# The last sums of c11 on GpSimd instead of VectorE at the end of each half of an MLP with seven-product multiplication

## The reference, cut to what matters

```python
hn = rmsnorm(h, norm2_g[l])
ff = jnp.square(jax.nn.relu(jnp.einsum('bsd,df->bsf', hn, w_mlp_in[l])))
h = h + jnp.einsum('bsf,fd->bsd', ff, w_mlp_out[l])
return rmsnorm(h, final_norm_g)
```

## Time and profile before

| what | value |
|---|---|
| time, median of 3 runs | 2180.83 us (2179.65 to 2180.89) |
| the profiled execution, its own time | 2179.79 us |
| its span, first to last instruction | 2178.1 us |
| PE busy | 2142.7 us (98%) |
| DVE busy | 1610.7 us (74%) |
| POOL busy | 872.0 us (40%) |
| ACT busy | 807.8 us (37%) |

### The profile page before, as it was taken

The page is one execution under the profiler, slowest core; times in us unless marked ns, Lnnn a source line. Parts: engine busy times, 40 slices in busy tenths (PEclk is TensorE's granted clock), DMA queues, the critical chain, the costliest instruction groups (busy, mean ns, idle before and its releaser), DMA issues.

```text
span 2178.1 us, 29249 instructions
## 1 busy us (share of the span) xinstructions
PE 2142.7 (98%) x9880; PEld 1755.8 (81%) x9880; DVE 1610.7 (74%) x2602; ACT 807.8 (37%) x1220; POOL 872.0 (40%) x860
## 2 busy tenths in 40 slices
PE   7999999999999999999999999999999999999998
PEld 6787788788878878888888888878788888888877
DVE  2899877887669853778678678786786786786785
ACT  4445554335165360323323333234223323323314
POOL 5553364044134432344344344434443533533521
PEclk9999999999999999999999999999999999999999
DMA  6884467355644647112112112132321121121111
GB/s 215 275 260 134 144 217 266 130 172 173 231 154 160 233 169 250 39 39 76 39 39 76 39 39 77 58 110 82 138 77 39 39 77 39 39 77 39 39 58 78
DMA packets 149822, 252.35 MB, mean 116 GB/s; under 512 B 9936, under 2 KB 91888, under 8 KB 149744
## 3 DMA queue, kind: packets, MB, share of 16 engines
q1 hardware_dynamic: 149744, 251.34, 35.0%
HBM read 205.17 MB, written 46.14 MB: 115 GB/s over the span
## 4 chain that ended last, share of the span: by engine, by line
PE 90%; DVE 4%; ACT 0%; issue 0%; POOLq 0%; POOL 0%; DVEq 0%; ACTq 0%
PE acc L75 22%; PE acc L77 22%; PE acc L76 22%; PE acc L2093 3%; PE acc L2095 3%; PE acc L2094 3%; PE acc L2138 2%; DVE h_sb L1617 2%; PE acc L1936 2%; PE acc L1937 2%; PE acc L1938 2%; PE acc L2053 1%; PE acc L2051 1%; PE acc L2052 1%; PE acc L1854 1%; PE acc L2118 1%
## 5 line engine op out<-in xcount | busy, mean ns | idle before, releaser
L954 POOL TENSOR_TENSOR up_lo<-raw_a,up_hi 128x1024 fp32r<-128x1024 f32 x62 | 149.5, 2413 | 544.2 <-ACT up_hi L1160 544.2
L1505 DVE SCALAR_TENSOR_TENSOR acc<-u_sb,cw_col,acc 128x512 f32<-128x512 f32 x464 | 313.2, 751 | 0.4
L76 PE MATMUL acc<-dn_lo,ff_hi 128*128 128x512 f32 x728 | 283.5, 389 | 0.0
L77 PE MATMUL acc<-dn_hi,ff_lo 128*128 128x512 f32 x728 | 283.5, 389 | 0.0
L75 PE MATMUL acc<-dn_hi,ff_hi 128*128 128x512 f32 x728 | 283.5, 389 | 0.0
L1658 DVE TENSOR_TENSOR h_sb<-acc,h_sb 128x512 f32<-128x512 f32 x416 | 269.3, 688 | 0.0
L1663 DVE TENSOR_TENSOR relu<-relu 128x512 f32<-128x512 f32 x104 | 74.3, 714 | 208.8 <-ACT relu L1260 208.8
L75 PE MATMUL acc<-xT_hi,wt 128*128 128x512 f32 x512 | 207.4, 405 | 1.5 <-ACT q_sb L1345 1.5
L75 PE MATMUL acc<-xT_hi,up_hi 128*128 128x512 f32 x512 | 200.1, 391 | 1.9 <-DVE h_sb L1582 1.1
L77 PE MATMUL acc<-xT_hi,wt 128*128 128x512 f32 x512 | 199.9, 390 | 0.0
L76 PE MATMUL acc<-xT_lo,wt 128*128 128x512 f32 x512 | 199.7, 390 | 0.0
(11 more groups left out here) (238 smaller groups left out, 4659.5 us busy)
## 6 DMA issues: line engine op xcount, KB each, us to landing
wt<-w_kept SPq DMA_DIRECT2D x168, 512.0 KB, 3.3
raw_a<-in_w_mlp_in SPq DMA_DIRECT2D x64, 512.0 KB, 6.9
raw_b<-in_w_mlp_out SPq DMA_DIRECT2D x62, 512.0 KB, 3.7
w_kept<-wt SPq DMA_DIRECT2D x48, 512.0 KB, 4.5
w_raw<-in_w_in SPq DMA_DIRECT2D x32, 256.0 KB, 3.6
h_sb<-h_dram SPq DMA_DIRECT2D x16, 512.0 KB, 7.0
res_sb<-in_x SPq DMA_DIRECT2D x7, 1024.0 KB, 5.5
h_dram<-res_sb SPq DMA_DIRECT2D x7, 1024.0 KB, 6.3
```

Source lines behind the costliest of these rows:

```text
L76: nc.tensor.matmul(out, w_hi, x_lo, start=False, stop=False)
L77: return nc.tensor.matmul(out, w_lo, x_hi, start=False, stop=last)
L954: nc.gpsimd.tensor_tensor(m_lo[i], raw[i], m_hi[i].bitcast(F32), ALU.subtract).then_inc(up_lo_ok, 1)
L1505: nc.vector.scalar_tensor_tensor(out=y_sb[:, j, :] if k == TAPS - 1 else bank, in0=u_sb[:, j, k:k + BLK], scalar=cw_col[:, j, k:k + 1], in ...
```

## The change

In the step after the seven-product ones POOL does the three combinations of `c11`, 12 instructions of 128 x 512 per half, right behind its two `dn_lo` and ahead of its two `up_lo`. It waits for the last of the seven-product adds (`seven_add`), which DVE has counted, and each second and third instruction of a tile for the one before it (a new semaphore, `c11_ok`). DVE does the other five combinations: 0 and 1 ahead of the first square as before, one each behind tiles 0 and 1, none behind tiles 2 and 3, and one tile of the last combination instead of two after each of the first four pairs of adds. The adds 0, 2, 4 and 6 wait for their tile of `c11`. SP waits for both semaphores ahead of the next half's loads.

```diff
+            def finish_c11(f, i):
+                half = f // NF
+                if i == 0:
+                    pool.wait_ge(seven_add, NS * (half + 1) * MT)
+                for n, (other, op) in enumerate(((m1_sum, ALU.add), (m4_sum, ALU.add), (m5_sum, ALU.subtract))):
+                    if n > 0:
+                        pool.wait_ge(c11_ok, half * 12 + 3 * i + n)
+                    nc.gpsimd.tensor_tensor(c11[i], c11[i], other[i], op).then_inc(c11_ok, 1)
...
@@ GpSimd, step(f) @@
                 for i in range(FT):
                     down_low(f, i)
                 if after_seven(f):
+                    for i in range(4):
+                        finish_c11(f, i)
                     for i in range(FT):
                         up_low(f + 1, i)
...
@@ SyncE @@
-                    sp.wait_ge(comb_ok, 32)
+                    sp.wait_ge(comb_ok, 20)
+                    sp.wait_ge(c11_ok, 12)
...
@@ VectorE, adds(f) @@
-                    if after_seven(f) and n in (0, NG // 2):
-                        dve.wait_ge(comb_ok, f // NF * 32 + (24 if n == 0 else 32))
+                    if after_seven(f) and n % 2 == 0 and t < 4:
+                        dve.wait_ge(c11_ok, f // NF * 12 + 3 * t + 3)
+                    if after_seven(f) and n == 0:
+                        dve.wait_ge(comb_ok, f // NF * 20 + 8)
+                    if after_seven(f) and n == NG // 2:
+                        dve.wait_ge(comb_ok, f // NF * 20 + 20)
...
                     if n % 2 == 1 and after_seven(f) and t < 4:
-                        combine(f, 6, [t])
-                        combine(f, 7, [t])
+                        combine(f, 4, [t])
...
@@ VectorE, combine(f, k, rows) @@
-                into, other, op = ((c22, c12, ALU.add), (c12, m5_sum, ALU.add), (c11, m1_sum, ALU.add),
-                                   (c11, m4_sum, ALU.add), (c11, m5_sum, ALU.subtract), (c22, c21, ALU.subtract),
+                into, other, op = ((c22, c12, ALU.add), (c12, m5_sum, ALU.add), (c22, c21, ALU.subtract),
                                    (c21, m4_sum, ALU.add), (c22, m1_sum, ALU.add))[k]
...
-                        dve.wait_ge(comb_ok, f // NF * 32 + (4 * (k - 1) + i + 1 if k < 6 else 24))
+                        dve.wait_ge(comb_ok, f // NF * 20 + (4 * (k - 1) + i + 1 if k < 4 else 16))
...
@@ VectorE, step(f) @@
-                    if after_seven(f):
+                    if after_seven(f) and i < 2:
                         combine(f, 2 + i, range(4))
```

More of the change, by code:

```diff
@@ L466, in hybrid_block @@
         comb_ok = sem("comb_ok")
+        c11_ok = sem("c11_ok")
         fin_ok = sem("fin_ok")
```

## The result

| what | before | changed |
|---|---|---|
| time, median | 2180.86 us | 2197.62 us (2197.49 to 2197.71, 4 runs) |
| ratio, 95% interval | | 1.0074 (1.0062 to 1.0087) |
| the profiled execution, its own time | 2179.79 us | 2197.71 us |
| span | 2178.1 us | 2196.0 us |
| POOL busy | 872.0 us | 911.3 us |

The change makes the kernel 0.74% slower; 2196.4 us was forecast. DVE has 24 instructions less and is busy 7 us longer: its instructions take longer beside POOL's. The lines have moved by the added code: 1617 is now 1632, 1631 is 1646, 1635 is 1650, 1582 is 1599, 1936 to 1938 are 1951 to 1953; POOL's new sums are line 971.

A forecast was written before the change was run, and what follows sets the result against it. PE, busy 98%, was taken as the bound, held by DVE's third `ff_lo` and first add. Per half 12.0 - 4.2 = 7.8 us later; 2179.8 + 15.6 = 2195.4, plus 1.0 for the median: 2196.4 us, range 2191 to 2202.

The forecast's parts named there:

- What bounds the kernel: End of each half: PE stops for DVE, 1.6 us ahead of `down` group 0, 4.2 ahead of group 4, then slow clock.
- DVE's own instructions: At unchanged length, 16 combination instructions still precede the third `ff_lo`; 8 fewer before the first add, worth up to 4.2 us.
- T1: Instant of DVE's third `ff_lo`, gate of PE's group 0; forecast 12.0 us later per half.
- Price of one alternation: DVE and POOL SBUF instructions take turns: pair 1.26 + 0.41 = 1.67 us, 1.07 lost per POOL instruction.
- All twelve ahead of T1, one wait covered: All 12 POOL sums meet DVE before T1, losing 12.8 us; POOL's turn covers one `ff_hi` wait, minus 0.8.
- POOL's own wait at nothing: POOL's wait on `c11_ok` costs 0.07 us, within DVE's 0.41, so nothing; if on top, net 9.1 per half.
- Rival B: DVE gets two turns to one of POOL's: 1.5 us later per half, 2183.8 us; chance 0.12.
- Slow clock, no change: PE's half-clock restart after a stop: one before, one after; bounds -4.0 us for both halves to +4.0.
- Rival C: Dearer alternation, 1.86 to 1.9 us per pair, with a longer slow clock: 2202 to 2205 us; chance 0.12.
- Rival A: DVE loses nothing to POOL; 4.2 us stops and slow clock go, 12.4 us faster, 2168.4 us; chance 0.08.
- Rival D: No difference: DVE's loss equals the 4.2 us, only 4 or 5 of 12 sums meeting DVE; chance 0.04.
- The sign that line 1617 would take 1.7: DVE's combinations, first 16 instructions of the step, should take about 1.7 us each beside POOL's new line.

The follow-up runs named there:

- e6_spread: Kernel before, nothing on POOL: all 32 combination instructions per half on DVE, reordered, 16 of them between the adds; 2165.28 us, ratio 0.9926.
- e3_none: Changed kernel with the sums of c11 left out on both POOL and DVE; 2168.20 us, ratio 0.9942.
- e7_one_ahead: Kernel before with one combination (c21 += m4, 4 instructions) moved from between the adds to ahead of the first add, on DVE; 2185.58 us, ratio 1.0019.
- e1_memset: Changed kernel with POOL's 12 sums of c11 per half replaced by memsets of the same tiles, which read nothing; 2168.15 us, ratio 0.9941.
- e4_by_sum: Changed kernel with POOL's 12 sums reordered so each waits for the one four places back, not the one just before; 2196.84 us, ratio 1.0072.
- e5_pool_late: Changed kernel with the sums still on POOL but behind both up_lo, each tile's three behind the add into that tile; 2170.76 us, ratio 0.9953.

## Why the prediction was right

- **What bounds the kernel** (the third `ff_lo` and the first add): shown. e6_spread brings both forward and gets 15.9 us, where 15.6 had been worked out (2 x 5.8 and 4.0 of slow clock). By halves it is 7.5 and 8.3, worked out 7.4 and 8.2.
- **DVE's own instructions**: T1 unmoved and the stop ahead of group 4 gone if POOL cost nothing. e3_none shows both and gives 2168.2 against 2168.4. The sums from between the adds are worth nothing: e7_one_ahead shows it from the other side.
- **Price of one alternation**: 1.67 was worked out, 1.70 measured, in every experiment with POOL's sums ahead of T1. The lost time per sum is 1.10 instead of 1.07; less the covered 0.8 that makes 12.4, and T1 came 12.2 later (12.0 forecast). The price with DVE's whole 0.60 held, an estimate of 1.86, is too high here; what the missing 0.16 of the pair is, no run shows. In the Trainium skill ("SBUF — State Buffer", section "Who interferes with whom") the words that the other engine fully blocks for the whole instruction are written of VectorE's 2-port modes; of a VectorE instruction with two SBUF inputs it says that it contends with a GpSimd instruction that reads SBUF and not with one that only writes it. e1_memset agrees with the second: beside 12 memsets VectorE stayed at 0.60. The waits here agree with the first in kind (2.81 per pair beside `dn_lo`), and the 1.70 is less than its words would give.
- **All twelve ahead of T1, one wait covered**: as in DVE's timeline; the covered wait at 1417.49 and the twelfth pair at the second square, as counted.
- **PE**: one stop of 13.6 us (13.6 forecast), none ahead of group 4; the adds, the loads and `up_lo` stayed hidden.
- **POOL's own wait at nothing**: e4_by_sum shows it. Rival B (two DVE turns to one of POOL's), which it would have started, didn't come.
- **Slow clock, no change**: 12 slow matmuls instead of 8 in the first half, 0.8 us more, and 11 instead of 12 in the second, 0.2 less: inside its bounds.
- Rival C's price (1.86 or more) wasn't reached. Rival A was wrong as to the reads and right in its number. Rival D would have needed 4 or 5 sums to meet DVE; all 12 did.
- The sign that line 1617 would take 1.7 in all of the first 16 instructions was too wide: the first three lie beside `dn_lo` as before, nine take 1.70, and of the last four only one is stretched, beside `up_lo` (4.63 together).

The forecast missed by 1.2 us, and a part of that closeness is luck. In the profiled executions it is 17.9 against 15.6, 2.3 more: 2 x 0.2 of T1, 0.8 less 0.2 of clock, and 1.3 ahead of the changed step, which no part of the change touches. The medians hide 1.1 of it, since the execution profiled before the change lay 1.0 below its median and the one after 0.1 above.

## What to carry to other kernels

Before a sum goes from VectorE to GpSimd, look in the trace for a VectorE instruction with two SBUF operands beside a GpSimd one that reads SBUF: if it is stretched, moved work costs VectorE more (here 1.1 us) than doing it (0.6 us). Where VectorE reads PSUM its instructions aren't stretched. That moving a sum pays even there, no run shows: e5_pool_late gains 10.4 us on the kernel before, but e6_spread gets 15.9 by moving sums behind the same instants on VectorE. Ask first which of the sums must be done before the instant that another engine waits for; here 16 of 32 could wait until between the adds, and that order alone beat both divisions of the work that were tried.

## What the runs showed of the hardware that was not expected

The alternation settled at 1.70 us per pair for 128 x 512 float32, whether or not GpSimd had to wait for its own result. VectorE's share in it was 1.70 - 1.26 = 0.44, less than the 0.60 that its instruction takes alone. Memsets on GpSimd left VectorE's two-operand instructions at 0.60 to 0.61, where GpSimd's subtractions a few microseconds earlier had stretched them to 2.8.
